# Fewer plain pairs ahead of the seven-product pairs in three SwiGLU layers, and another order of VectorE's list

## The chip, the cores and the metric

The kernel runs on one core of a Trainium2 chip. The metric is the time on the device of one execution, in microseconds (us). Engines are TensorE (PE in the profile), VectorE (DVE), ScalarE (ACT), GpSimd (POOL) and SyncE (SP), which issues the DMAs of the weights.

## What is computed

Two transformer-like blocks over 512 tokens of width 1024, all in float32. Three SwiGLU layers of width 2816 in them take most of the time, and the change touches only those:

```python
def swiglu(x, w_gate, w_up, w_down):
    return (jax.nn.silu(x @ w_gate) * (x @ w_up)) @ w_down

h = h + 0.5 * swiglu(rmsnorm(h, ffn1_norm[l]), ...)   # "g1"
...                                                    # attention branches, gates, projection
h = h + 0.5 * swiglu(rmsnorm(h, ffn2_norm[l]), ...)   # "g2"
...                                                    # convolution and pooling block
h = h + swiglu_2(rmsnorm_2(h, g_ffn[l]), ...)          # "g3"
```

## The kernel before

Each float32 operand is split into a high part (a cast to the rounded type fp32r) and a low part (the value less the high one), and a product is the sum of high x high, low x high and high x low. Weights come in units of 128 x 1024 (one weight chunk for 128 outputs), 512 KB each, through a ring of four slots (`RING`): SyncE loads `raw`, ScalarE casts it to `wh` (`high`, L1204), GpSimd subtracts to `wl` (`low_part`, L487). A slot is loaded again when TensorE has signalled `unit_done` for it.

A layer's gate and up projections have 22 pairs of units (`FC`), one gate and one up unit for each 128 columns. They are done in two ways (`gate_up`):

- The first `PLAINS[name]` pairs are plain: 2 units x 8 chunks x 3 products = 48 matmuls of 512 columns (L620 to L622). VectorE takes the two sums out with `plain_taken` (L1755, L1758), ScalarE does `silu`, VectorE multiplies in `plain_hidden` (L1765).
- The other pairs are mixed: gate and up share seven products instead of eight half-size ones, over combined inputs and combined weights. In `mixed_pair` TensorE does, in order, E, NG, B21, ND, the next pair's B11, B22 and NF, 72 matmuls, 60 of 256 columns and 12 of 512 (L732 to L749). The very first B11 is `first_product`, which stands inside the last plain unit, behind its fifth chunk.

Mixed pairs need combined inputs. For each of four chunks k VectorE makes eight half-width tiles in `mixed_input` (L1773 to L1781), ScalarE casts seven of them (`mixed_input` there, L1329), and VectorE subtracts (`mixed_input_low`, L1786). This is done beside the plain pairs. The combined weights are made pair by pair in VectorE's `frame(p)`: it makes the sums and low parts that pair p+1 needs (L1817, L1819, L1826, L1837, L1844, L1846, L1849, L1858) and puts the products of pair p together (L1823, L1829, L1833, L1840, L1854, L1862). L1840 signals `ff_gate`, without which NF of that pair does not start: its columns of the bank are still being read. `finish` (L1796) makes the hidden chunk. `frame(-1)` stands ahead of the loop and makes the weights of pair 0. ScalarE has a `frame` of its own with the casts and the copies of products (L1334, L1339, L1367); GpSimd does, for each pair, two half-width low parts (`pair_low`, L528, behind L1849) and one quarter (`next_quarter`, L540, behind ScalarE's cast).

Each engine works through its list strictly in the order in which the code writes it; semaphores tie the lists together. There is no planner.

## Time and profile before

| | us |
|---|---|
| median of 3 runs | 1737.55 (1736.27 to 1737.61) |
| profiled execution | 1736.21 |
| its span | 1734.4 |
| mixed part of g1, 16 pairs, first E to the end of the last pair | 77.0 to 235.9 |
| mixed part of g2, 17 pairs | 947.4 to 1116.0 |
| mixed part of g3, 17 pairs | 1431.7 to 1600.5 |

The profiled execution is one run of the program; the profile's times are counted from the start of its span. The granted clock of TensorE was full (0.998 of full speed on the mean). The timeline lists instructions in order of time; a matmul's own duration overlaps the next one's, so the pace of TensorE is read from the distance between starts. The same holds for VectorE to a small extent: instructions of 128 x 512 show 0.68 us and start 0.60 us apart. In brackets stands how long the engine was idle before an instruction and what ended that.

### The profile page before, as it was taken

How to read it: one execution, taken by the hardware profiler on the slowest of the kernel's cores; microseconds unless marked ns; L12 is line 12 of the kernel's file. 1: busy time of each engine (PE TensorE's matmuls, PEld its weight loads, DVE VectorE, ACT ScalarE, POOL GpSimd, SP SyncE). 2: the span in 40 equal slices, each digit the busy share in tenths (PEclk: the TensorE clock that was granted, in tenths of full speed). 3: DMA queues.
4: the chain of work that ended last, by engine and by line, in shares of the span. 5: the costliest groups of instructions: out<-in, count | busy, mean ns of one | idle time of the engine just before them, and what ended most of it. 6: DMA issues, size and time to landing. Idle time of an engine off the chain costs nothing.

```text
span 1734.4 us, 27783 instructions
## 1 busy us (share of the span) xinstructions
PE 1720.8 (99%) x9696; PEld 1454.7 (84%) x9696; DVE 1206.8 (70%) x1809; ACT 876.1 (51%) x1486; POOL 783.0 (45%) x423
## 2 busy tenths in 40 slices
PE   9999999999999999999999999999999999999998
PEld 7899988888888777788888999988866889999887
DVE  6898984278867885236469899843785598998532
ACT  6455552266554477785344555522425445555222
POOL 2344354467565433325453344544533534435443
PEclk9999999999999999999999999999999999999999
DMA  5333333322333221112323333332361323333222
GB/s 178 98 108 102 104 104 96 127 93 88 110 110 113 64 72 50 50 49 86 97 92 95 104 109 104 103 97 97 104 146 61 97 85 107 103 106 109 97 98 73
DMA packets 50518, 168.54 MB, mean 97 GB/s; under 512 B 6264, under 2 KB 7032, under 8 KB 50304
## 3 DMA queue, kind: packets, MB, share of 16 engines
q1 hardware_dynamic: 47088, 161.34, 29.9%
q10 hardware_dynamic: 3344, 6.05, 1.3%
q8 instruction: 55, 0.90, 0.2%
q14 instruction: 31, 0.25, 0.0%
HBM read 161.84 MB, written 2.11 MB: 95 GB/s over the span
## 4 chain that ended last, share of the span: by engine, by line
PE 92%; DVE 4%; issue 2%; ACT 1%; POOL 1%; DMA 0%; POOLq 0%; SPq 0%; ACTq 0%; DVEq 0%
PE bank L620 16%; PE bank L622 16%; PE bank L621 16%; PE bank L746 8%; PE bank L914 7%; PE bank L732 6%; PE bank L734 5%; PE bank L735 5%; PE bank L744 3%; PE bank L959 2%; PE bank L985 2%; PE bank L1087 1%; PE bank L976 1%; PE bank L749 1%; DVE input_low L1691 1%
## 5 line engine op out<-in xcount | busy, mean ns | idle before, releaser
L487 POOL TENSOR_TENSOR weights_low<-raw_weights,weights_high 128x1024 fp32r<-128x1024 f32 x192 | 470.1, 2453 | 558.4 <-ACT weights_high L1204 530.5
L1204 ACT CAST weights_high<-raw_weights 128x1024 fp32r<-128x1024 f32 x244 | 254.1, 1045 | 296.9 <-DMA raw_weights<-weights 278.0
L528 POOL TENSOR_TENSOR weights_low<-raw_weights,weights_high 128x512 fp32r<-128x512 f32 x100 | 149.6, 1518 | 286.4 <-DVE weights_low L1849 286.4
L620 PE MATMUL bank<-input_high,weights_high 128*128 128x512 f32 x624 | 246.2, 395 | 2.4 <-DVE input_low L1691 1.7
L621 PE MATMUL bank<-input_high,weights_low 128*128 128x512 f32 x624 | 243.1, 390 | 0.0
L622 PE MATMUL bank<-input_low,weights_high 128*128 128x512 f32 x624 | 243.1, 390 | 0.0
L732 PE MATMUL bank<-input_mixed,weights_high 128*128 128x256 f32 x600 | 171.9, 287 | 0.0
L735 PE MATMUL bank<-input_mixed,weights_high 128*128 128x256 f32 x600 | 169.2, 282 | 0.0
L746 PE MATMUL bank<-input_mixed,weight_sum_high 128*128 128x512 f32 x400 | 148.9, 395 | 0.0
L620 PEld LDWEIGHTS bank<-input_high,weights_high 128*128 128x128 f32 x624 | 117.2, 188 | 30.7 <-issue 5.0
L622 PEld LDWEIGHTS bank<-input_low,weights_high 128*128 128x128 f32 x624 | 117.1, 188 | 24.8
L621 PEld LDWEIGHTS bank<-input_high,weights_low 128*128 128x128 f32 x624 | 117.2, 188 | 23.2 <-issue 0.2
L1339 ACT CAST weight_sum_high<-weight_sum 128x512 fp32r<-128x512 f32 x150 | 93.3, 622 | 81.7 <-PE bank L746 48.8
L620 PE MATMUL bank<-hidden_high_mid,weights_high 128*128 (+1 forms) x336 | 130.7, 389 | 0.0
L621 PE MATMUL bank<-hidden_high_mid,weights_low 128*128 (+1 forms) x336 | 130.7, 389 | 0.0
L732 PEld LDWEIGHTS bank<-input_mixed,weights_high 128*128 128x128 f32 x600 | 113.8, 190 | 5.0 <-DVE bank L1840 3.1
L735 PEld LDWEIGHTS bank<-input_mixed,weights_high 128*128 128x128 f32 x600 | 114.0, 190 | 0.0
L734 PE MATMUL bank<-input_mixed,weights_low 128*128 128x256 f32 x400 | 113.0, 283 | 0.0
L622 PE MATMUL bank<-hidden_low_first,weights_high 128*128 (+1 forms) x288 | 112.1, 389 | 0.0
L1741 DVE SCALAR_TENSOR_TENSOR residual<-bank,residual 128x512 f32<-128x512 f32 x39 | 26.8, 686 | 108.5 <-PE bank L622 108.4
L1334 ACT COPY product_copies<-bank 128x256 f32<-128x256 f32 x150 | 66.4, 443 | 53.8 <-PE bank L746 47.6
L622 PE MATMUL bank<-hidden_low_rest,weights_high 128*128 128x512 f32 x240 | 93.4, 389 | 0.0
(330 smaller groups left out, 4340.3 us busy)
## 6 DMA issues: line engine op xcount, KB each, us to landing
raw_weights<-weights SPq DMA_DIRECT2D x294, 512.0 KB, 3.6
out_t<-out_t SPq DMA_DIRECT2D x8, 256.0 KB, 2.1
residual<-x_t SPq DMA_DIRECT2D x6, 256.0 KB, 5.9
glu_stacked<-glu_padded ACTq DMA_DIRECT2D x24, 64.0 KB, 4.6
glu_stacked<-glu_padded SPq DMA_DIRECT2D x24, 64.0 KB, 4.7
mem_in<-mem_t ACTq DMA_DIRECT2D x1, 1024.0 KB, 4.9
tile<-forget_sums ACTq DMA_DIRECT2D x4, 256.0 KB, 3.5
raw_weights<-weights SPq DMA_DIRECT2D x3, 256.0 KB, 5.8
```

The lines of the kernel that those rows point to most:

```text
L487: pool.tensor_tensor(wl[:, u % RING, :], raw[:, u % RING, :], wh[:, u % RING, :].bitcast(F32), ALU.subtract).then_inc(low_done, 1)
L528: pool.tensor_tensor(wl[:, u % RING, w], raw[:, u % RING, w], wh[:, u % RING, w].bitcast(F32), ALU.subtract).then_inc(low_done, 1)
L620: pe.matmul(out, wh[:, u % RING, w], rh, start=start, stop=False)
L621: pe.matmul(out, wl[:, u % RING, w], rh, start=False, stop=False)
L622: return pe.matmul(out, wh[:, u % RING, w], rl, start=False, stop=stop)
L732: pe.matmul(out, high[:, w], xmix[k][:, of, 0:HALF], start=first and k == 0, stop=False, skip_group_check=not first)
L734: pe.matmul(out, low[:, w], xmix[k][:, of, 0:HALF], start=False, stop=False, skip_group_check=not first)
L735: mm = pe.matmul(out, high[:, w], xmix[k][:, of, HALF:], start=False, stop=k == 3, skip_group_check=not first)
L746: mm = pe.matmul(out, high[:, w], xmix[k][:, of, :], start=first and k == 0, stop=k == 3, skip_group_check=not first)
L914: mm = pe.matmul(bank[g % 2][:, :], (wl if part == 1 else wh)[:, u % RING, w], (xl if part == 2 else xh)[:, k, :], start=(k == 0 and part ...
L1204: act.copy(wh[:, u % RING, :], raw[:, u % RING, :]).then_inc(high_done, 1)
L1339: act.copy(dst, src).then_inc(sem("sum_high"), 1)
```

## The change

`PLAINS` goes from 6, 5, 5 to 5, 4, 4, so each layer has one plain pair less and one mixed pair more. With four plain pairs `pair_bank` puts the mixed pairs in banks 6/7 and 0/1 in turn (in 0/1 and 2/3 with an odd number, as before), and `first_product` no longer waits for the last `plain_hidden`. The eight tiles of a combined input are put in the order in which TensorE's products use them, and those of chunks 2 and 3 are cast and subtracted in two pieces, `EARLY` (three tiles: B11, E, NG) and `LATE` (four: B21, ND, B22, NF). In g2 and g3 VectorE does the late pieces inside `frame(-1)`, and all of plain pairs 2 and 3 behind it. In the loop the adds that lead to `ff_gate` (L1833, L1829, L1840) move ahead of L1826 and L1837. The diff, cut:

```diff
+PLAINS = {"g1": 5, "g2": 4, "g3": 4}
+EARLY, LATE = slice(0, 3), slice(3, 7)
 HALF = S // 2

-ND_OF, E_OF, NF_OF, NG_OF, B21, B22, B11, B12 = range(8)
+B11, E_OF, NG_OF, B21, ND_OF, B22, NF_OF, B12 = range(8)


 N_GU, N_DN, N_IN, N_BR, N_WO, N_IN2, N_WO2 = 2 * FC, FC, len(IN_STEPS) + GATES, 12, 8, 12, 8
...
+            return 2 * ((n + p) % 2) if n % 2 else 6 * (p % 2 == 0)
+
         def halves_of(tile):
             return tile.rearrange("p (a n) -> p a n", n=HALF)

...
-                pe.wait_ge(sem("xmix_low"), before(name, 4) + 4)
-                pe.wait_ge(sem("ff_hidden"), before(name, FC) + plain - 1)
+                pe.wait_ge(sem("xmix_low"), before(name, 6) + 4)
+                if plain % 2:
+                    pe.wait_ge(sem("ff_hidden"), before(name, FC) + plain - 1)
                 pe.wait_ge(sem("quarter_low"), pairs_before(name, 1) + 1)
-                mixed_product(bank[2 * (plain % 2)][:, 0:HALF], wh[:, up % RING, 0:S], quarter_low, B11).then_inc(sem("products"), 1)
+                mixed_product(bank[pair_bank(name, 0)][:, 0:HALF], wh[:, up % RING, 0:S], quarter_low, B11).then_inc(sem("products"), 1)
...
+                if p == 0:
+                    pe.wait_ge(sem("xmix_low"), before(name, 6) + 6)
                 pe.wait_ge(low_done, at(u + 1, 2))
...
                     high(u, i=i)
+                    if p < 0 and not plain % 2:
+                        mixed_input(3, LATE)
                     if p >= 0:
...
@@ -1387,18 +1399,9 @@
                     mixed_input(1)
                     silu(1)
                     high(u0 + 7)
-                    mixed_input(2)
-                    if plain > 4:
-                        high(u0 + 8)
-                    mixed_input(3)
-                    silu(2)
-                    if plain > 4:
-                        high(u0 + 9)
-                        silu(3)
-                    if plain > 5:
-                        high(u0 + 10)
-                        high(u0 + 11)
-                        silu(4)
+                    mixed_input(2, EARLY)
+                    mixed_input(2, LATE)
+                    mixed_input(3, EARLY)
...
                     high(8)
-                    mixed_input(2)
+                    mixed_input(2, EARLY)
                     high(9)
+                    mixed_input(2, LATE)
+                    mixed_input(3, EARLY)
+                    mixed_input(3, LATE)
                     silu(2)
-                    high(10)
-                    mixed_input(3)
                     silu(3)
-                    high(11)
-                    silu(4)
                 frame(-1)
-                copy_product(copies[:, 0, 0, :], bank[2 * (plain % 2)][:, 0:HALF], 1)
+                copy_product(copies[:, 0, 0, :], bank[pair_bank(name, 0)][:, 0:HALF], 1)
+                if not plain % 2:
+                    silu(plain - 2)
                 silu(plain - 1)
                 looped = mixed // 2 * 2 - 2
...
+                    if p < 0 and not plain % 2:
+                        mixed_input_low(2, 4, LATE)
                     if now:
                         dve.wait_ge(unit_done, at(u0 + 2 * (plain + p) + 1, 2))
                         dve.wait_ge(sem("copied"), at(copied + 3 * p + 1, 3))
                         dve.tensor_tensor(up_out[:, 0:HALF], bank[4][:, 0:HALF], copies[:, c, 0, :], ALU.add
                                           ).then_inc(sem("partial"), 1)
-                    if more:
-                        dve.tensor_tensor(gate[:, 0:S], gate[:, 0:S], up[:, 0:S], ALU.add).then_inc(sem("sums"), 1)
-                    if now:
-                        dve.wait_ge(sem("partial"), at(pairs_before(name, 3) + 3 * p + 1, 3))
-                        dve.tensor_tensor(up_out[:, 0:HALF], bank[4][:, HALF:S], up_out[:, 0:HALF], ALU.add)
-                    if now:
                         dve.wait_ge(sem("products"), at(products + 5 * p + 4, 5))
                         dve.wait_ge(sem("copied"), at(copied + 3 * p + 3, 3))
                         dve.tensor_tensor(bank[b][:, HALF:S], bank[b][:, 0:HALF], copies[:, c, 2, :], ALU.add
                                           ).then_inc(sem("partial"), 1)
+                        dve.wait_ge(sem("partial"), at(pairs_before(name, 3) + 3 * p + 1, 3))
+                        dve.tensor_tensor(up_out[:, 0:HALF], bank[4][:, HALF:S], up_out[:, 0:HALF], ALU.add)
                     if more:
-                        dve.wait_ge(sem("sums"), sum_at(4 * p + 6))
-                        dve.tensor_tensor(s4[:, :], sums[1][:, :], up[:, S:2 * S], ALU.add).then_inc(sem("sums"), 1)
+                        dve.tensor_tensor(gate[:, 0:S], gate[:, 0:S], up[:, 0:S], ALU.add).then_inc(sem("sums"), 1)
                     if now:
                         dve.wait_ge(sem("partial"), at(pairs_before(name, 3) + 3 * p + 2, 3))
                         dve.tensor_tensor(bank[b][:, HALF:S], bank[b][:, HALF:S], copies[:, c, 3, :], ALU.add
                                           ).then_inc(sem("ff_gate"), 1)
                     if more:
+                        dve.wait_ge(sem("sums"), sum_at(4 * p + 6))
+                        dve.tensor_tensor(s4[:, :], sums[1][:, :], up[:, S:2 * S], ALU.add).then_inc(sem("sums"), 1)
                         dve.wait_ge(sem("sum_high"), sum_at(4 * p + 6))
                         dve.tensor_tensor(sum_l[1][:, :], sums[1][:, :], sum_h[1][:, :].bitcast(F32), ALU.subtract
                                           ).then_inc(sem("sum_low"), 1)
                         dve.tensor_tensor(sum_l[0][:, :], sums[0][:, :], sum_h[0][:, :].bitcast(F32), ALU.subtract
                                           ).then_inc(sem("sum_low"), 1)
+                        if p < 0 and not plain % 2:
+                            mixed_input_low(3, 6, LATE)
                         dve.wait_ge(sem("sum_high"), sum_at(4 * p + 7))
                         dve.tensor_tensor(wl[:, (u + 1) % RING, 0:S], gate[:, 0:S], wh[:, (u + 1) % RING, 0:S].bitcast(F32),
                                           ALU.subtract).then_inc(sem("sum_low"), 1)
...
                     plain_taken(1)
                 plain_hidden(1)
                 mixed_input(2)
-                mixed_input_low(1)
+                mixed_input_low(1, 2)
                 if not u0:
                     plain_taken(2)
                 mixed_input(3)
+                mixed_input_low(2, 3, EARLY)
+                mixed_input_low(3, 5, EARLY)
+                if not u0:
+                    mixed_input_low(2, 5, LATE)
+                    mixed_input_low(3, 6, LATE)
+                    plain_hidden(2)
+                    plain_taken(3)
+                    plain_hidden(3)
+                frame(-1)
                 if u0:
                     plain_taken(2)
-                mixed_input_low(2)
-                plain_hidden(2)
-                if not u0:
-                    plain_taken(3)
-                mixed_input_low(3)
-                if not u0:
-                    plain_hidden(3)
-                for c in range(3 if u0 else 4, plain - 1):
-                    plain_taken(c)
-                    plain_hidden(c)
-                frame(-1)
+                    plain_hidden(2)
                 plain_taken(plain - 1)
                 plain_hidden(plain - 1)
                 looped = mixed // 2 * 2 - 2
```

## Rows read from the trace of the kernel before

**Rows 1.** The page, part 1: busy time of each engine, share, instructions.

```profile
PE 1720.8 (99%) x9696; PEld 1454.7 (84%) x9696; DVE 1206.8 (70%) x1809; ACT 876.1 (51%) x1486; POOL 783.0 (45%) x423
```

**Rows 2.** Line L732: what its engine waited for before it: us, times.

```profile
  DVE bank L1840: 3.1, 20
```

**Rows 3.** Timeline, TensorE, first stage: start us, us, engine, line, operation [idle before].

```profile
59.70 0.39 PE L622 MATMUL bank<-input_low,weights_high 128*128 128x512 f32 x1
...
73.30 0.39 PE L622 MATMUL bank<-input_low,weights_high 128*128 128x512 f32 x1
...
73.52 0.28 PE L732 MATMUL bank<-input_mixed,weights_high 128*128 128x256 f32 x1
...
77.01 0.28 PE L732 MATMUL bank<-input_mixed,weight_sum_high 128*128 128x256 f32 x1
```

**Rows 4.** Timeline, TensorE, second stage, columns as in the group above.

```profile
943.88 0.28 PE L732 MATMUL bank<-input_mixed,weights_high 128*128 128x256 f32 x1
...
947.36 0.28 PE L732 MATMUL bank<-input_mixed,weight_sum_high 128*128 128x256 f32 x1
...
955.86 0.28 PE L732 MATMUL bank<-input_mixed,weights_high 128*128 128x256 f32 x1
...
957.29 0.28 PE L732 MATMUL bank<-input_mixed,weight_sum_high 128*128 128x256 f32 x1
...
1105.72 0.30 PE L732 MATMUL bank<-input_mixed,weights_high 128*128 128x256 f32 x1
...
1116.00 0.50 PE L620 MATMUL bank<-hidden_high_first,weights_high 128*128 128x512 f32 x1
```

**Rows 5.** Timeline, VectorE, second stage: last mixed input to the loop.

```profile
926.71 0.74 DVE L1773 SCALAR_TENSOR_TENSOR input_sums<-residual,vectors,bank 128x512 f32<-128x512 f32 x1
...
928.27 2.30 DVE L1777 TENSOR_TENSOR input_sums<-input_sums 128x512 f32<-128x512 f32 x1
...
932.60 2.02 DVE L1786 TENSOR_TENSOR input_mixed<-input_sums,input_mixed 128x1792 fp32r<-128x1792 f32 x1
...
935.13 4.22 DVE L1786 TENSOR_TENSOR input_mixed<-input_sums,input_mixed 128x1792 fp32r<-128x1792 f32 x1
...
947.19 0.68 DVE L1755 TENSOR_TENSOR tile<-bank,token_factor 128x512 f32<-128x512 f32 x1
...
948.57 1.66 DVE L1765 TENSOR_TENSOR hidden_rest<-tile,tile 128x512 f32<-128x512 f32 x1
...
951.31 0.69 DVE L1817 TENSOR_TENSOR weight_sum<-raw_weights 128x512 f32<-128x512 f32 x1 [1.09 <-DMA raw_weights<-weights]
...
954.24 0.68 DVE L1837 TENSOR_TENSOR weight_sum<-weight_sum,raw_weights 128x512 f32<-128x512 f32 x1
...
954.84 0.43 DVE L1840 TENSOR_TENSOR bank<-bank,product_copies 128x256 f32<-128x256 f32 x1
...
1105.09 0.43 DVE L1840 TENSOR_TENSOR bank<-bank,product_copies 128x256 f32<-128x256 f32 x1
```

**Rows 6.** Timeline, GpSimd, the same stretch of the second stage.

```profile
927.62 2.39 POOL L487 TENSOR_TENSOR weights_low<-raw_weights,weights_high 128x1024 fp32r<-128x1024 f32 x1 [4.23 <-ACT weights_high L1204]
...
941.64 1.46 POOL L540 TENSOR_TENSOR quarter_low<-raw_weights,weights_high 128x512 fp32r<-128x512 f32 x1 [4.17 <-ACT weights_high L1204]
...
946.84 2.84 POOL L528 TENSOR_TENSOR weights_low<-raw_weights,weights_high 128x512 fp32r<-128x512 f32 x2 [3.73 <-DVE weights_low L1849]
```

**Rows 7.** Timeline, ScalarE, second stage: one whole cast of a unit.

```profile
940.53 1.03 ACT L1204 CAST weights_high<-raw_weights 128x1024 fp32r<-128x1024 f32 x1
```

**Rows 8.** Timeline, VectorE, first stage, before its first frame.

```profile
50.69 0.74 DVE L1773 SCALAR_TENSOR_TENSOR input_sums<-residual,vectors,bank 128x512 f32<-128x512 f32 x1
...
53.39 2.52 DVE L1779 SCALAR_TENSOR_TENSOR input_sums<-input_sums 128x256 f32<-128x256 f32 x1
...
61.96 2.88 DVE L1765 TENSOR_TENSOR hidden_rest<-tile,tile 128x512 f32<-128x512 f32 x1
...
68.99 0.69 DVE L1817 TENSOR_TENSOR weight_sum<-raw_weights 128x512 f32<-128x512 f32 x1 [2.16 <-DMA raw_weights<-weights]
```

40 lines of the change are left out of this document (21 added, 19 removed).

## The prediction

> **What bounds the kernel now.** I read the busy times first: TensorE 99%, VectorE 70% [rows 1]. The reader is to see that TensorE hardly idles over the whole, so the first question is how many matmuls go. Next I looked at what ended TensorE's idle time at L732, the line that opens NF: VectorE's L1840, 3.1 us in all [rows 2]. Then the timelines of the three places where plain pairs give way to mixed ones. There the share of 70% misleads. In g2 VectorE has no gap from 926.71 until the 1.09 us in front of L1817 at 951.31 [rows 5], while the same stretch of g1 has 2.16 us free in front of its first frame [rows 8]. So each layer's head has two limits, TensorE's matmuls and VectorE's list, and the change moves the first by a whole plain pair.
>
> **Matmul count.** Sixty matmuls of 512 columns start within 73.30 - 59.70 = 13.60 us, 0.2267 each [rows 3]. A plain pair has 48: 10.88 us. A mixed pair takes 957.29 - 947.36 = 9.93 us from E to E where nothing holds it [rows 4]. Each layer swaps one for the other: 0.95 us less, 2.85 us in three layers. Everything ahead of the last plain pair stands as it was, so the first E is wanted 10.88 us earlier.
>
> **The loop.** L1840 falls due once a pair. From its start at 954.84 to 1105.09 are 15 pairs, 10.017 us each [rows 5], against TensorE's 9.93. It is slower from the first pair on, when TensorE doesn't yet wait: L1840(0) ends at 955.27 and NF(0) starts at 955.86 [rows 4, 5]. So VectorE's list has a period of its own, and TensorE runs into it after some six pairs; that gives the 3.1 us. I see what makes it: an instruction of VectorE with two inputs in SBUF doesn't run beside one of GpSimd. L1777, about 0.7 us alone, took 2.30 (to 930.57) while GpSimd's low part ran from 927.62 to 930.01, and L1765 took 1.66, not 0.69, beside `pair_low` [rows 5, 6]. Per pair VectorE gives way to such instructions three times. The new order drops none of these instructions, so I keep 10.017. It does put L1840 ahead of L1837, 0.60 us (954.24 to 954.84) [rows 5]; L1829 and L1833 merely change places with L1826. So `ff_gate` comes 0.60 us sooner once, not in each pair: at most 0.6 per layer. New waits it could bring: L1833 needs ND, which ends 7.1 us after NF starts, about 1 us before VectorE gets there; ScalarE's cast behind L1826 comes 0.66 later, with two more VectorE instructions before its reader L1849. I cost both at nothing in the steady loop, at up to 0.2 us in a layer's first pairs.
>
> **g1.** VectorE between 50.69 and 68.99 [rows 8]: the last mixed input, its low parts, two pairs taken out, one wait. Of these 18.30 us go: 2.16 idle; three instructions of one pair, 1.8 (taken and hidden of pair 4 move behind the frame); 2.1 in L1779 (2.52 against 0.42) and 2.2 in L1765 (2.88 against 0.68), both held by low parts of units 10 and 11, which now are made as quarters and halves; 0.4 in L1777 likewise. Added: two instructions by the splits, 0.14, and a wait of 0.1 for the cast. The frame starts at about 60.5. With one hold of 1.0 by the quarter its fifth instruction ends at about 64.8, before E at 77.01 - 10.88 = 66.13 [rows 3]. The first B11 is due at 73.52 - 10.88 = 62.64, the quarter ends at about 62.45: hidden, with little to spare. So TensorE gains the whole pair: -10.88 + 9.93 - 0.5 (the order: 0.6 less 0.1 for one more pair of the slow period) = **-1.45 us**. If the cover fails by 0.5 us, it is -1.
>
> **g2.** The work is cut in another way here, late pieces in the frame and pairs 2 and 3 behind it, but all of it still lies ahead of `frame(0)`, so the order hardly matters for L1840(0). I sum from 926.71, where nothing has changed, to L1817 of `frame(0)` at 951.31: 24.60 us [rows 5]. Minus 1.8 for one pair taken and hidden (three times 0.60); minus 1.6 in L1777 (2.30 against 0.7) and 2.2 in the second L1786 (4.22 against 2.02), since units 8 and 9 no longer have whole low parts; minus the idle 1.09. Plus 0.14 for two more instructions, 0.1 for a cast, and 1.0 for the next quarter, which now meets VectorE at L1819, as large as the hold of L1765 (1.66 against 0.69) [rows 5]; in the old list it met the idle time. That is 19.15 us: L1817 in effect at 945.86, and L1840 ends 3.53 + 0.43 - 0.60 = 3.36 later, at 949.2. NF(0) is wanted at 955.86 - 10.88 = 944.98 [rows 4]. It is 4.2 us late, and the lateness stays, as VectorE's period is no shorter than TensorE's.
>
> Where TensorE would stand meanwhile: 0.6 at the first B11 (quarter done at 933.6, wanted at 933.0); 0.4 at E (the frame is longer by a late piece, and the copy of B11 waits behind ScalarE's list); 0.8 at B21, which needs GpSimd's half behind L1849, itself behind the second late piece; 3.0 at ND, for a copy that stands in ScalarE's list behind the silu of pair 3 and a cast of 1.03 [rows 7], and that silu waits for VectorE's L1755 at 942.9. The four waits are bounds of the same lateness: together 4.8 us.
>
> End of the layer: before, L1840(15) ends at 1105.52, NF(15) starts 0.20 later, the layer ends 10.28 behind that [rows 4, 5]. Now there are 16 periods behind 949.2: 949.2 + 160.3 = 1109.5, end at 1119.9 against 1116.00: **+4.0 us**. Bounds: if VectorE lost nothing to the quarter and the halves at the start (1.0 each at L1819, at the hidden of pair 2 and at the sum in front), it is 3 less, +1.0; if ScalarE's late copy costs its 4.8 on top of a full loop loss (17 x 0.087 less the 0.5 of slack, 1.0, against 0.9 now), it is 4.8 - 0.95 + 0.1 = +4.0 again; if both chains add a hold of a whole 1.0 and 0.5 more, +5.5. I take +4.0, since each term has a row of the same shape.
>
> The Trainium skill, "SBUF — State Buffer", section "Who interferes with whom", says that VectorE with two SBUF inputs and GpSimd share one pair of ports, and that whoever issues first keeps it for the whole instruction. This trace agrees: L1777 ends 0.56 us after the GpSimd instruction that it waited for [rows 5, 6]. No row shows the other order in the loop, L1817 ahead of the quarter. By the page the quarter would then wait and hold L1819 in its turn, the period would stay at 10.02 and g2 at +4.0; without it g2 could be rival 2's +3.0.
>
> **g3** repeats g2: its last mixed input starts at 1411.03, its L1817 at 1435.72, its first E at 1431.67, distances within 0.1 us of g2's. **+4.0 us** (same bounds).
>
> **Sum.** -1.45 + 4.0 + 4.0 = +6.55 us. Against the profiled execution's 1736.21 (span 1734.4 and 1.8 around it) it gives 1742.8; that execution lies 1.3 below the median, and the median moves to **1744.1 us**, 0.38% slower. A measurement can tell about 0.2% (3.5 us) from no change.
>
> **The rivals.**
> 1. VectorE's head late, as above: 1744.1, within 1741 to 1748. For it: the missing gap in VectorE's timeline. Chance 0.55.
> 2. The same head, but the new order brings the loop's period down to TensorE's 9.93, say because a weight load that lands sooner lets L1817 run before the quarter. Then g2 and g3 end at TensorE's pace behind NF(0) at 949.8: 949.8 + 16 x 9.93 + 10.28 = 1119.0, +3.0 each, and g1 gives -1.95: 1741.6. Against it: the same instructions share the ports whoever goes first. Chance 0.10.
> 3. The holds at the head mostly fall away, because GpSimd's halves and VectorE's instructions pass each other: +1.0 each, 1738.1, no change to be measured. Chance 0.13.
> 4. The other side: VectorE's head isn't what NF(0) waits for. The mechanism would be that the late pieces and the two pairs behind the frame take work out of the path of the first E, and that TensorE's start is all that counts, with `ff_gate` early enough. It decides if L1840(0) ends by 944.98, that is 4.2 us ahead of my sum. Then 2.85 and most of the 3.1 go: 1737.55 - 5.9 = 1731.6, or 1734 with the slow period left. For it: TensorE's first E and B11 are covered nearly in full. Against it: nothing takes VectorE's work away. Chance 0.13.
> 5. Worse: ScalarE's late copy and silus push the loop's first pairs as well, or g1 fails too (its quarter has 0.2 us to spare): +5.5 each and 0 in g1, 1748.5. Chance 0.09.
>
> **How the numbers follow.** Slower by over 0.2%: rivals 1, 2 and 5, less the corner of 1 and 2 near 1741: 0.72. Within 0.2%: rival 3 and that corner: 0.15. Faster: rival 4: 0.13. The range of 8 in 10 goes from rival 3's 1738.0 to 1748.0, near rival 5's; it leaves out rival 4 and part of 5.
>
> **What would show it right or wrong.** Right: in g2 and g3 VectorE without a gap until L1817 of `frame(0)`, and that one starting without a wait for a DMA; L1840(0) near 949 + the 1.45 us that g1 takes off the clock before; TensorE's gaps at ND, B21 and B11 of the first mixed pair, some 4.8 us a layer, with a copy and L1849 as their releasers; L1840 still 10.02 apart; g1 with no gap at its first B11 and E, its mixed part at 168 to 169 us. Wrong: a gap on VectorE in front of `frame(0)`, or L1840 less than 9.95 apart, or first mixed pairs of 9.93 us in g2. My sum would fail first if a hold by GpSimd falls elsewhere than I put it, since these are 1 us apiece and six of them stand in it.

## The result and the profile after

The changed kernel takes 1744.13 us (median of 5 runs, 1743.52 to 1746.64), the kernel before beside it 1737.28 (5 runs, 1735.66 to 1737.61). The ratio is 1.0045 [1.0034, 1.0057], so it is 6.85 us slower; the forecast was 1744.1, in a range of 1738.0 to 1748.0. The profiled execution took 1743.5 (span 1741.6), TensorE's clock 0.998 of full on the mean.

The page, part 1, of the kernel after (answers to [rows 1]):

```profile
PE 1719.7 (99%) x9768; PEld 1455.8 (84%) x9768; DVE 1242.1 (71%) x1851; ACT 884.6 (51%) x1513; POOL 782.5 (45%) x426
```

TensorE is busy 1.1 us less in a span that is 7.2 us longer. What L738 (L732 before) waited for, us and times, answers to [rows 2]; this list counts a matmul and its weight load both:

```profile
  ACT product_copies L1344: 11.9, 6
...
  DVE bank L1842: 1.6, 10
  POOL quarter_low L546: 1.3, 4
```

VectorE's L1842 (L1840 before), which led the list with 3.1, has sunk to 1.6; in front stands a copy of ScalarE that wasn't there at all. Timeline of TensorE, second stage (answers to [rows 4]): first B11, E, B21, ND, NF, the second pair's E, the end of the layer.

```profile
932.62 0.36 PE L738 MATMUL bank<-input_mixed,weights_high 128*128 128x256 f32 x1 [0.49 <-POOL quarter_low L546]
...
936.35 0.39 PE L738 MATMUL bank<-input_mixed,weight_sum_high 128*128 128x256 f32 x1
...
940.11 0.50 PE L752 MATMUL bank<-input_mixed,weights_high 128*128 128x512 f32 x1 [0.67 <-POOL weights_low L534]
...
944.38 0.39 PE L738 MATMUL bank<-input_mixed,weights_high 128*128 128x256 f32 x1 [2.61 <-ACT product_copies L1344]
...
948.73 0.28 PE L738 MATMUL bank<-input_mixed,weights_high 128*128 128x256 f32 x1
...
950.17 0.28 PE L738 MATMUL bank<-input_mixed,weight_sum_high 128*128 128x256 f32 x1
...
1119.21 0.50 PE L626 MATMUL bank<-hidden_high_first,weights_high 128*128 128x512 f32 x1 [0.37 <-DVE hidden_low_first L1917]
```

From E to E the first pair takes 950.17 - 936.35 = 13.82 us, where [rows 4] has 9.93. The same in the first stage (answers to [rows 3]), where nothing waits:

```profile
63.12 0.28 PE L738 MATMUL bank<-input_mixed,weights_high 128*128 128x256 f32 x1
...
66.61 0.28 PE L738 MATMUL bank<-input_mixed,weight_sum_high 128*128 128x256 f32 x1
```

VectorE, second stage (answers to [rows 5]). From 925.69 to L1822 (L1817 before) of `frame(0)` no instruction waits for anything:

```profile
925.69 0.74 DVE L1777 SCALAR_TENSOR_TENSOR input_sums<-residual,vectors,bank 128x512 f32<-128x512 f32 x1
...
927.25 0.69 DVE L1781 TENSOR_TENSOR input_sums<-input_sums 128x512 f32<-128x512 f32 x1
...
931.36 1.67 DVE L1824 TENSOR_TENSOR weight_sum<-weight_sum,raw_weights 128x512 f32<-128x512 f32 x1
...
940.21 1.65 DVE L1769 TENSOR_TENSOR hidden_rest<-tile,tile 128x512 f32<-128x512 f32 x1
941.78 0.68 DVE L1759 TENSOR_TENSOR tile<-bank,token_factor 128x512 f32<-128x512 f32 x1
...
943.77 0.68 DVE L1822 TENSOR_TENSOR weight_sum<-raw_weights 128x512 f32<-128x512 f32 x1
944.49 1.66 DVE L1824 TENSOR_TENSOR weight_sum<-weight_sum,raw_weights 128x512 f32<-128x512 f32 x1
...
947.67 0.42 DVE L1842 TENSOR_TENSOR bank<-bank,product_copies 128x256 f32<-128x256 f32 x1
...
1098.04 0.42 DVE L1842 TENSOR_TENSOR bank<-bank,product_copies 128x256 f32<-128x256 f32 x1
```

The three of 1.65 to 1.67 us, otherwise 0.69, meet a GpSimd instruction and wait for it, which is called a hold below: a quarter, `pair_low` and a quarter. The last two lines are 15 periods of 10.025 us. ScalarE at the same place: the silu of pair 3, which waits for VectorE's L1759, then a whole cast and the two copies that ND waits for.

```profile
942.49 0.63 ACT L1335 ACTIVATE tile<-tile 128x512 f32<-128x512 f32 x1 [2.32 <-DVE tile L1759]
943.03 1.03 ACT L1214 CAST weights_high<-raw_weights 128x1024 fp32r<-128x1024 f32 x1
943.96 0.85 ACT L1344 COPY product_copies<-bank 128x256 f32<-128x256 f32 x2
```

Where the time went, by the distance between the ends of the layers' mixed parts:

| stretch | before | after | difference | forecast |
|---|---|---|---|---|
| first plain unit of g1 to its end | 207.35 | 206.17 | -1.18 | -1.45 |
| end of g1 to end of g2 | 880.13 | 884.04 | +3.91 | +4.0 |
| end of g2 to end of g3 | 484.51 | 488.36 | +3.85 | +4.0 |

The first plain unit itself started 0.48 later in this execution (29.00 against 28.52), ahead of all that was changed. The three rows sum to +6.58. The row of g2 holds 0.32 us that were gained between the layers, where nothing was changed: g1 ended 0.70 earlier than before, g2's last mixed input (L1777 at 925.69, L1773 at 926.71) came 1.02 earlier. Counted from that instruction, g2 costs 4.23 us; g3, in the same way, 3.89.

### The profile page after: what moved, and what is told of

It reads as the page before. It is cut to its first block, busy times and chain, and to the rows that moved or that the text cites. A ratio compares the mean times of both kernels' runs of the same rounds, so it can differ in the third digit from the quotient of the medians.

```text
span 1741.6 us, 28200 instructions
## 1 busy us (share of the span) xinstructions
PE 1719.7 (99%) x9768; PEld 1455.8 (84%) x9768; DVE 1242.1 (71%) x1851; ACT 884.6 (51%) x1513; POOL 782.5 (45%) x426
## 4 chain that ended last, share of the span: by engine, by line
PE 88%; DVE 7%; issue 2%; ACT 1%; POOL 1%; DMA 0%; POOLq 0%; SPq 0%; ACTq 0%
PE bank L626 14%; PE bank L627 14%; PE bank L628 14%; PE bank L752 8%; PE bank L924 8%; PE bank L738 6%; PE bank L740 6%; PE bank L741 6%; PE bank L750 3%; PE bank L969 2%; PE bank L995 2%; PE bank L1097 1%; PE bank L986 1%; PE bank L755 1%; DVE input_low L1695 1%
## 5 line engine op out<-in xcount | busy, mean ns | idle before, releaser
L493 POOL TENSOR_TENSOR weights_low<-raw_weights,weights_high 128x1024 fp32r<-128x1024 f32 x186 | 455.5, 2453 | 532.0 <-ACT weights_high L1214 503.3
L534 POOL TENSOR_TENSOR weights_low<-raw_weights,weights_high 128x512 fp32r<-128x512 f32 x106 | 158.6, 1517 | 300.9 <-DVE weights_low L1855 300.9
L626 PE MATMUL bank<-input_high,weights_high 128*128 128x512 f32 x576 | 227.5, 395 | 2.8 <-DVE input_low L1695 2.2
L627 PE MATMUL bank<-input_high,weights_low 128*128 128x512 f32 x576 | 224.5, 390 | 0.0
L628 PE MATMUL bank<-input_low,weights_high 128*128 128x512 f32 x576 | 224.4, 390 | 0.0
L738 PE MATMUL bank<-input_mixed,weights_high 128*128 128x256 f32 x636 | 181.9, 286 | 6.2 <-ACT product_copies L1344 5.2
L741 PE MATMUL bank<-input_mixed,weights_high 128*128 128x256 f32 x636 | 179.4, 282 | 0.0
L752 PE MATMUL bank<-input_mixed,weight_sum_high 128*128 128x512 f32 x424 | 157.9, 395 | 0.0
L626 PEld LDWEIGHTS bank<-input_high,weights_high 128*128 128x128 f32 x576 | 108.2, 188 | 29.0 <-issue 5.5
L738 PEld LDWEIGHTS bank<-input_mixed,weights_high 128*128 128x128 f32 x636 | 120.6, 190 | 11.8 <-ACT product_copies L1344 5.9
L628 PEld LDWEIGHTS bank<-input_low,weights_high 128*128 128x128 f32 x576 | 108.1, 188 | 23.0
L741 PEld LDWEIGHTS bank<-input_mixed,weights_high 128*128 128x128 f32 x636 | 120.7, 190 | 0.0
```

Source lines behind the costliest of these rows:

```text
L493: pool.tensor_tensor(wl[:, u % RING, :], raw[:, u % RING, :], wh[:, u % RING, :].bitcast(F32), ALU.subtract).then_inc(low_done, 1)
L534: pool.tensor_tensor(wl[:, u % RING, w], raw[:, u % RING, w], wh[:, u % RING, w].bitcast(F32), ALU.subtract).then_inc(low_done, 1)
L626: pe.matmul(out, wh[:, u % RING, w], rh, start=start, stop=False)
L627: pe.matmul(out, wl[:, u % RING, w], rh, start=False, stop=False)
L628: return pe.matmul(out, wh[:, u % RING, w], rl, start=False, stop=stop)
L738: pe.matmul(out, high[:, w], xmix[k][:, of, 0:HALF], start=first and k == 0, stop=False, skip_group_check=not first)
```

## The experiments

The kernel before, run beside them, had a median of 1736.81 (beside order_only, old_order, five and five_quarter), 1737.3 (beside after_quarter, thin_quarter, more_vector and head_before_frame) and 1736.98 (beside the other four). Where a stage is named, the numbers are distances as in the table above.

**order_only** is the kernel before with the new list in the loop alone: the adds that lead to `ff_gate` ahead of L1826 and L1837.

```diff
                     if more:
-                        dve.wait_ge(sem("sums"), sum_at(4 * p + 6))
-                        dve.tensor_tensor(s4[:, :], sums[1][:, :], up[:, S:2 * S], ALU.add).then_inc(sem("sums"), 1)
+                        dve.tensor_tensor(gate[:, 0:S], gate[:, 0:S], up[:, 0:S], ALU.add).then_inc(sem("sums"), 1)
                     if now:
                         ...
                                           ).then_inc(sem("ff_gate"), 1)
                     if more:
+                        dve.wait_ge(sem("sums"), sum_at(4 * p + 6))
+                        dve.tensor_tensor(s4[:, :], sums[1][:, :], up[:, S:2 * S], ALU.add).then_inc(sem("sums"), 1)
```

> The kernel before with the new order of VectorE's list in the loop alone (plain pairs 6, 5, 5). My theory: the order gives 0.6 us once per layer and leaves L1840's period at 10.02 us, so TensorE's waits at L732 fall from 3.1 to about 1.3 us and the time by 1.8 us, to 1735.5. Rival: the order brings the period to TensorE's 9.93, all waits go, minus 3.1 us. Second rival: a new wait at L1833 eats the gain, no change.

Measured: 1736.13 us (11 runs), ratio 0.9996 [0.9987, 1.0005]. End of g1 to end of g2: 0.32 shorter, g2 to g3: equal. The period of `ff_gate` stays at 10.01 to 10.05 but for single pairs. NF of g2 begins to wait at about the ninth pair, not the sixth, so the list does give the slack of 0.6, but 0.3 of it is lost again at a B11 for which the quarter came late, in a pair where the weight sum went ahead of it. In g1 the weights for the second frame landed 1.4 later, VectorE was late from there, and the stretch from the first E to the end of the layer is 1.03 longer than before; why the weights landed later isn't shown. VectorE's timeline, order_only:

```profile
82.45 0.69 DVE L1817 TENSOR_TENSOR weight_sum<-raw_weights 128x512 f32<-128x512 f32 x1 [3.38 <-DMA raw_weights<-weights]
```

From the first E to the layer's end g2 is 0.16 shorter and g3 equal. Up to the last E they gain 0.25 and 0.33; from there to the end they lose 0.09 and 0.33, for a reason shown below with the forecast's term for the list. So the list is worth 0 to 0.2 a layer here, less than the forecast's 0.6.

**old_order** is the other half: the kernel after with the old list, so the edit above the other way round.

> The changed kernel with the old order in the loop. My theory: g2 and g3 each end 0.6 us later and g1 0.5, since VectorE's list bounds them, so plus 1.7 us on the changed kernel, 1745.8. Rival (order pays nothing where the head is late): 1744.1. Second rival (order changes the period): plus 3 or more.

Measured: 1746.14 us (5 runs), ratio 1.0053 [1.004, 1.0067], 2.0 above the kernel after. g1 ends 0.28 later and g2 to g3 is 0.54 longer, at full clock: that is the list's share (0.45 in either from the first E to the end). g1 to g2 is 1.5 longer, and there TensorE's clock fell. Windows from ND of the first mixed pair to the second E, in g2 and in g3: length, busy time of PE, PEld, DVE, ACT and POOL, then the granted clock:

```profile
944.77:952.07 7.30, 7.30 (x44) 7.13 (x45) 6.96 (x13) 3.70 (x7) 2.25 (x2) 0.77 0.06 25
1434.77:1440.67 5.90, 5.90 (x44) 5.60 (x45) 5.87 (x11) 3.60 (x7) 1.23 (x1) 1.00 0.10 37
```

The same 44 matmuls take 7.30 at 0.77 and 5.90 at 1.00, 0.12 of which is a wait for VectorE.

**five** leaves five plain pairs in g2 and g3 too, with the split inputs and the new list; pairs 2 to 4 and the late pieces stand as in g1, ahead of the frame for pairs 2 and 3 (VectorE's list is changed in the same way as ScalarE's, shown here).

```diff
-PLAINS = {"g1": 5, "g2": 4, "g3": 4}
+PLAINS = {"g1": 5, "g2": 5, "g3": 5}
...
+                    high(u0 + 8)
                     mixed_input(3, EARLY)
+                    mixed_input(3, LATE)
+                    silu(2)
+                    high(u0 + 9)
+                    silu(3)
```

> The changed kernel with five plain pairs in all three layers: g2 and g3 go back to five, with the split inputs and the new order, g1 stays at five. My theory: the loss of the change is all in going to four pairs in g2 and g3; here g1 keeps its 0.7 us and g2 and g3 gain 0.6 each by the order: 1735.4, that is 8.7 below the changed kernel. Rival: the split of the casts costs by itself in g2 and g3: 1737 or more.

Measured: 1734.58 us (11 runs), ratio 0.9987 [0.9978, 0.9996], g1 to g2 0.24 and g2 to g3 0.26 shorter than before. All of the loss is in going to four plain pairs; with five, g1 keeps its gain and VectorE waits 1.13 (g2) and 0.91 (g3) for a DMA ahead of `frame(0)` again. From the first E to the end g2 and g3 are 0.11 longer and 0.20 shorter than before, so the split inputs and the new list together change little there.

**five_quarter** adds to five one wait on GpSimd: the quarter goes behind VectorE's weight sum instead of ahead of it.

```diff
+                        pool.wait_ge(sem("sums"), pairs_before(name, 4) + at(4 * q + 1, 8))
                         pool.tensor_tensor(quarter_low[:, :], ...
```

> As the run with five pairs in all layers, and GpSimd's quarter waits for L1822 of the same frame, so that VectorE's first sum always takes the ports ahead of it. In the changed kernel's trace that happened twice by chance, and the period of L1842 was 9.82 there, not 10.02. My theory: period below 9.93 in every pair, TensorE's waits at NF go, minus 1.2 more: 1734.2. Rival: B11 then waits for the quarter in every pair, some 0.3 us each, plus 10 us or more. Second rival: the two short periods were chance, no change against 1735.4.

Measured: 1787.69 us, ratio 1.0296 [1.0282, 1.031]. The theory fell. The waits close a ring through four lists: NF frees a weight slot, the DMA fills it, the sum waits for the DMA, the quarter for the sum, B11 for the quarter, NF stands behind B11. Timelines of VectorE, GpSimd and TensorE, five_quarter:

```profile
181.32 0.69 DVE L1828 TENSOR_TENSOR weight_sum<-raw_weights 128x512 f32<-128x512 f32 x1 [2.11 <-DMA raw_weights<-weights]
182.09 1.77 POOL L547 TENSOR_TENSOR quarter_low<-raw_weights,weights_high 128x512 fp32r<-128x512 f32 x1 [2.90 <-DVE weight_sum L1828]
184.00 0.38 PE L739 MATMUL bank<-input_mixed,weights_high 128*128 128x256 f32 x1 [1.14 <-POOL quarter_low L547]
```

A pair then takes 10.9 to 11.4 us, 11.1 on the mean. **after_quarter** puts the same wait into the kernel after; it was meant to tell whether the quarter ahead of the sum costs VectorE its hold:

> The changed kernel with GpSimd's quarter behind L1822 of its frame. My theory: the head stays late by 4 us in g2 and g3, but the loop no longer loses to VectorE's period: minus 0.9 in g2 and g3 each, minus 0.5 in g1: 1741.8. Rival: B11 waits for the quarter, slower than 1744.1; in the head the quarter is late already, so it could cost up to 0.6 once in each layer.

Measured: 1796.86 us (4 runs), ratio 1.0342 [1.0324, 1.0359], the same ring: 10.7 to 11.3 us a pair, 11.0 to 11.1 on the mean of a layer. Neither run says what a hold costs.

**thin_quarter** does say it: all quarters but the first of each layer are cut to 8 columns, so most of that low part is left out of the output.

```diff
-                    pool.tensor_tensor(quarter_low[:, :], raw[:, u % RING, 0:S], ...
+                    n = 8 if q else S
+                    pool.tensor_tensor(quarter_low[:, 0:n], raw[:, u % RING, 0:n], ...
```

> The changed kernel, but every quarter except a layer's first is made over 8 columns instead of 512, so its low part is left out of the output. It takes one of GpSimd's three holds out of each pair. My theory (VectorE gives way to GpSimd's whole instruction): L1824 of frame(0) in g2 takes 0.69, not 1.66, L1842 is no longer the slower one and comes at TensorE's 9.93, and the time falls by some 2.3 us to 1741.8 (0.9 in g2 and g3, 0.5 in g1), no further, because ND of the first mixed pair still waits for ScalarE's copy. Rival (the period has another cause, say the weights' DMA): period 10.02 and 1744.1.

Measured: 1743.04 us (6 runs), ratio 1.0031 [1.0018, 1.0043]. The loop's period drops to 9.94 and g1 ends at 234.07, 1.1 earlier than after. In g2 and g3 the first L1825 after the head takes 0.69, not 1.66, yet the layers are no shorter than after's (884.21 and 488.72 against 884.04 and 488.36). In g2, from E to ND it is the same 8.02 as after's 8.03, since ND's copy waits for silu(3); from ND to the second E it is 1.50 more, at a fallen clock; from there to the end 1.29 less (167.75 against 169.04), of which 0.95 goes at NF in the loop and 0.34 behind the last E. Timeline, TensorE, and the two windows from ND to the second E, thin_quarter:

```profile
943.24 0.39 PE L739 MATMUL bank<-input_mixed,weights_high 128*128 128x256 f32 x1 [2.59 <-ACT product_copies L1345]
```

```profile
943.24:950.53 7.29, 7.29 (x44) 7.12 (x45) 6.02 (x13) 3.60 (x7) 0.89 (x2) 0.77 0.05 16
1431.95:1439.25 7.30, 7.30 (x44) 7.12 (x45) 5.64 (x13) 3.51 (x7) 0.43 (x2) 0.77 0.08 30
```

So two limits must be told apart, VectorE's list (V) and ScalarE's copy for ND (S). In the kernel after L1842(0) ends at 948.09 and NF starts at 948.73: `ff_gate` was ready 0.64 before NF, where an NF that waits for it starts 0.05 to 0.08 behind it. So this NF came late by TensorE's chain through ND; waiting for VectorE alone, it could have started some 0.6 sooner.

**more_vector** puts more of VectorE's instruction L1762 of `plain_taken` into the list: three in g2's third plain pair, one in g3's fourth and one in g1's fifth.

```diff
+                    for _ in range({("g1", 4): 1, ("g2", 2): 3, ("g3", 3): 1}.get((name, c), 0)):
+                        own(dve.tensor_tensor(tiles[2 + p][:, :], bank[2 * p + 1][:, :], rstd[:, :], ALU.mult))
```

> The changed kernel with VectorE instructions added that write nothing new (a copy of L1762 with a wait, about 0.72 us each, none with two SBUF inputs): three in g2 at the third plain pair, one in g3 at the fourth, one in g1 at the fifth. My theory (VectorE's list ahead of frame(0) sets the end of g2 and g3, and g1 has 0.87 us to spare): g2 plus 2.2, g3 plus 0.7, g1 nothing: 1747.0. Rival (TensorE's or ScalarE's waits at the head set it): less than half of that.

Measured: 1748.66 us (4 runs), ratio 1.006 [1.0043, 1.0077]. g1 is the same to 0.02, so VectorE has room there. g1 to g2 grew by 3.6, g2 to g3 by 1.23. The three took 2.13 us, but `plain_hidden(2)` came out of step with GpSimd and lost its hold of 1.0, so silu(3) and ND came only 1.22 later after E; another 2.37 went between ND and the second E, at a clock of 0.67. In g3 ND came no later after E (8.03), and between ND and the second E went 1.30, at a clock of 0.80. So the 2.2 and 0.7 that were expected of VectorE's list aren't seen: at equal clock it is 1.2 and nothing, and the run doesn't tell V from S. Timelines, VectorE and TensorE, and the window from ND to the second E, more_vector:

```profile
939.70 2.13 DVE L1763 TENSOR_TENSOR tile<-bank,token_factor 128x512 f32<-128x512 f32 x3
...
942.66 0.69 DVE L1771 TENSOR_TENSOR hidden_rest<-tile,tile 128x512 f32<-128x512 f32 x1
```

```profile
945.87 0.58 PE L738 MATMUL bank<-input_mixed,weights_high 128*128 128x256 f32 x1 [3.83 <-ACT product_copies L1344]
```

```profile
945.87:954.03 8.16, 8.16 (x44) 7.98 (x45) 6.98 (x13) 3.71 (x7) 2.06 (x2) 0.67 0.01 2
```

**head_before_frame** tests the forecast's sentence that the order of the head hardly matters: in g2 and g3 late pieces and pairs 2 and 3 go ahead of `frame(-1)`, on VectorE and on ScalarE.

```diff
-                frame(-1)
                 if u0:
                     plain_taken(2)
-                    plain_hidden(2)
-                plain_taken(plain - 1)
-                plain_hidden(plain - 1)
+                plain_hidden(2)
+                plain_taken(3)
+                plain_hidden(3)
+                frame(-1)
```

> The changed kernel with g2's and g3's heads in g1's arrangement: late pieces and plain pairs 2 and 3 ahead of frame(-1), nothing in or behind it; counts unchanged. My theory (the order of the head hardly matters for L1842 of frame(0), only its sum does): the first E is late by 5 us instead of none, ND no longer is, L1842 of frame(0) lies within 1 us of its place, and the time within 1.5 us of 1744.1. Rival (the late pieces and the pairs behind the frame are what keeps the loss small): plus 3 us or more for each of the two layers, 1750.

Measured: 1764.69 us (4 runs), ratio 1.0156 [1.0139, 1.0173]: 10.5 us a layer, and the sentence fell for the pairs. Not all of it is waiting: behind the waits of 6.53 and 5.03 the granted clock was 0.61 to 0.65 and then, in the first mixed pair, 0.83 to 0.85, and the matmuls took 4.2 us longer in g2 and 3.6 in g3 than the same ones before. ScalarE's cast for the quarter now stands behind silu(3), the quarter comes late, B11 stands in TensorE's list inside the last plain unit, and VectorE waits for that unit's bank before it makes the frame. Timelines of GpSimd, TensorE, VectorE and TensorE again, head_before_frame:

```profile
937.07 1.26 POOL L546 TENSOR_TENSOR quarter_low<-raw_weights,weights_high 128x512 fp32r<-128x512 f32 x1 [14.89 <-ACT weights_high L1214]
```

```profile
938.48 0.55 PE L738 MATMUL bank<-input_mixed,weights_high 128*128 128x256 f32 x1 [6.53 <-POOL quarter_low L546]
...
949.33 0.58 PE L738 MATMUL bank<-input_mixed,weight_sum_high 128*128 128x256 f32 x1 [5.03 <-ACT product_copies L1344]
```

```profile
944.34 0.69 DVE L1762 TENSOR_TENSOR tile<-bank,token_factor 128x512 f32<-128x512 f32 x1 [8.94 <-PE bank L628]
```

**late_ahead** moves the late pieces alone ahead of `frame(-1)`.

```diff
+                mixed_input_low(2, 5, LATE)
+                mixed_input_low(3, 6, LATE)
                 if not u0:
-                    mixed_input_low(2, 5, LATE)
-                    mixed_input_low(3, 6, LATE)
```

> The changed kernel, in g2 and g3 with the late pieces ahead of the first frame and only the plain pairs 2 and 3 behind it. A smaller test of the claim that the order of the head does not matter, after the arrangement with everything ahead of the frame cost 10 us a layer through a ring: pair 3 was awaited by the frame, and its last unit held the product that waited for the frame's cast. Here no ring: the first B11 starts 1 us later, E 1 us later, B21 as before, L1842 of frame(0) at its place within 0.3 us, and the time is the same, 1744. Rival: the late pieces inside the frame save what they shift, plus 1 us a layer.

Measured: 1744.29 us (4 runs), ratio 1.0039 [1.0023, 1.0054], as the kernel after. g2 to g3 is 0.33 longer at full clock; g1 to g2 is 1.46 longer, with a granted clock of 0.77 from ND to the second E. B11 and E come 0.5 and 1.2 later, the wait at ND is 0.2 shorter: the time is moved within the head. The 1 us a layer of the rival isn't there.

**taken_first** takes pair 3 out of its banks before `plain_hidden(2)`, so that silu(3) and the copy behind it come sooner, with the same number of instructions.

```diff
                     plain_taken(2)
-                    plain_hidden(2)
                 plain_taken(plain - 1)
+                if u0:
+                    plain_hidden(2)
                 plain_hidden(plain - 1)
```

> The changed kernel, in g2 and g3 with plain pair 3 taken out (L1759, L1762) ahead of the hidden of pair 2, so that ScalarE's silu of pair 3, its next cast and its copy come some 1.5 us sooner. VectorE's list keeps its sum. Theory V (VectorE's list sets the end of the layer): ND of the first mixed pair starts 1.5 us sooner, but L1842 of frame(0) stays at its place, 0.6 us ahead of NF before, and the layers end within 0.3 us of where they did: 1744. Rival S (ScalarE's late copy sets it): each of the two layers ends 1.5 us sooner, 1741.

Measured: 1740.11 us (11 runs), ratio 1.0016 [1.0007, 1.0025]; g1 to g2 1.43 and g2 to g3 1.16 shorter than after. The wait at ND goes from 2.61 to 0.86, but VectorE's end moved as well. Timelines of VectorE and of TensorE, taken_first:

```profile
940.96 1.27 DVE L1769 TENSOR_TENSOR hidden_rest<-tile,tile 128x512 f32<-128x512 f32 x2
...
946.07 0.42 DVE L1842 TENSOR_TENSOR bank<-bank,product_copies 128x256 f32<-128x256 f32 x1
```

```profile
942.36 0.38 PE L738 MATMUL bank<-input_mixed,weights_high 128*128 128x256 f32 x1 [0.86 <-ACT product_copies L1344]
```

Two of `plain_hidden` in 1.27 us, where one alone took 1.65: the hold by `pair_low` is gone, and L1842(0) comes 1.3 sooner against E. The run lands nearer S's 1741 than V's 1744, but both limits moved, so the total doesn't tell them apart. The stretches say more: from the first E to the end g2 is 1.45 and g3 1.22 shorter than after, near VectorE's 1.3 and not the copy's 1.75; NF(0) now starts 0.3 later against ND, and from the sixth pair on g2's TensorE waits for L1842.

**thin_taken** does both, thin quarters and pair 3 taken first.

> The thin quarters (8 columns behind a layer's first, so a low part is left out of the output) together with pair 3 taken out first. In the run with thin quarters alone TensorE's granted clock was 0.77 in the first mixed pair of g2 and g3, behind its wait at ND, and that hid what the quarters give. With the wait 1.5 us shorter I expect a clock of 1.00 there, L1843's period at TensorE's 9.93, and now the 1.3 us a layer of VectorE's period as well as the shorter head: g2 and g3 2 us each sooner than in the changed kernel, 1739.5. Rival: the clock falls here too, 1742.

Measured: 1736.43 us (10 runs), ratio 0.9996 [0.9987, 1.0005], better than the 1739.5 expected; g1 to g2 and g2 to g3 are 3.0 and 2.83 shorter than after, the period is 9.93 to 9.94, and the clock doesn't fall. Against taken_first that is 1.6 a layer in g2, 0.3 of it ahead of the second E and 1.29 behind it. So in the square of four (1744.1 after; 1743.0 thin; 1740.1 taken; 1736.4 both) thin quarters give 1.29 behind the second E with and without the swap, and the head nothing by themselves but 0.3 with the swap; the swap gives the head 1.75 up to ND in either case; and thin alone loses 1.5 again by the clock.

**five_gate_first** is five with L1842's add moved one place further ahead, before the add of the gate weights.

```diff
                                           ).then_inc(sem("ff_gate"), 1)
                     if more:
+                        dve.tensor_tensor(gate[:, 0:S], gate[:, 0:S], up[:, 0:S], ALU.add).then_inc(sem("sums"), 1)
+                    if more:
```

> The run with five plain pairs in all layers, and in the loop the add that signals ff_gate also ahead of the sum of the raw weights (L1845 behind L1848). My theory: ff_gate comes 0.6 us sooner once per layer, TensorE's remaining 0.8 us of waits at NF goes: 1733.9 against 1734.6. Rival: ScalarE's cast and copies behind that sum come 0.6 later and hold E of the next pair: no gain or slower.

Measured: 1734.13 us (11 runs), ratio 0.9982 [0.9973, 0.9991], the fastest of all and 10.0 below the kernel after. What L738 waited for, us and times:

```profile
...
  POOL quarter_low L546: 0.8, 3
```

VectorE is no longer in it, though its period is still 10.03: `ff_gate` of g2's first pair is ready at 953.39 for NF at 954.83, and each pair eats 0.1 of these 1.44 us. They don't run out (0.47 is the least in any layer), also because one pair in each layer is shorter by 0.2 on VectorE; but its B11 waits for the quarter there, and those pairs take TensorE 10.27 to 10.46 instead of 9.93. Against five the medians differ by 0.45, less than the intervals tell.

## Why the prediction was right, and where its steps were off

The mechanism was right: one plain pair less makes VectorE's list late at the head of g2 and g3, TensorE stands there for 4.8 us a layer, and g1 has room. That the total agrees so closely is luck: the three stretches were off by +0.27, -0.09 and -0.15 us, g2's row holds 0.32 that g2 didn't gain, the medians moved by 6.85 and five executions of the kernel lie 3.1 apart.

**Matmul count.** Right. In g1 the E of the first mixed pair comes 77.01 - 66.61 = 10.40 earlier, and 10.88 from the first plain unit's start, as summed.

**g1.** -1.18 against -1.45. B11 came at 62.64 by the clock of before (63.12 less the late start of 0.48), the forecast to the hundredth. The frame with its one hold is there too. VectorE, first stage (answers to [rows 8]):

```profile
60.92 0.68 DVE L1822 TENSOR_TENSOR weight_sum<-raw_weights 128x512 f32<-128x512 f32 x1
61.64 1.67 DVE L1824 TENSOR_TENSOR weight_sum<-weight_sum,raw_weights 128x512 f32<-128x512 f32 x1
...
70.76 0.83 DVE L1822 TENSOR_TENSOR weight_sum<-raw_weights 128x512 f32<-128x512 f32 x1 [0.87 <-DMA raw_weights<-weights]
```

VectorE waits 0.87 ahead of `frame(0)`: g1 still has room, g2 none. The term that was off is the new list's, -0.5: it is -0.36 up to the last E, where 0.2 went at one B11 (202.02, its quarter late), and +0.12 behind it.

**The new list's price, left out of the forecast.** The forecast took the layer's end as it was, 10.28 us behind the last NF. From the last E to the end of the layer it was 8.81 to 8.83; it is 8.93, 9.15 and 9.16 in g1, g2 and g3. In the new list VectorE's L1855, for which `pair_low` waits, starts 2.14 behind L1842, where L1849 started 1.54 behind L1840. GpSimd's work behind it comes later, its whole low part runs until 1118.60, and the first split of the hidden activations starts at 1118.14 and is held; the first matmul behind the layer waits 0.37 for it. Timelines of GpSimd and VectorE of the kernel after, and of VectorE before:

```profile
1116.20 2.40 POOL L493 TENSOR_TENSOR weights_low<-raw_weights,weights_high 128x1024 fp32r<-128x1024 f32 x1
1118.14 1.02 DVE L1917 TENSOR_TENSOR hidden_low_first<-hidden_first,hidden_high_first 128x512 fp32r<-128x512 f32 x1
```

```profile
1115.26 0.68 DVE L1912 TENSOR_TENSOR hidden_low_first<-hidden_first,hidden_high_first 128x512 fp32r<-128x512 f32 x1
```

Before, the same low part ended at 1115.14, just ahead. old_order, with the list of before, has 8.82 to 8.83 again, and so has thin_quarter (8.81), where VectorE isn't late.

**g2 and g3, VectorE's sum.** Right in size. By the clock of before (L1773 at 926.71, now 925.69, so 1.02 on top) L1842(0) ends at 949.11; the forecast was 949.2. Its parts are all there: L1781 at 0.69 without its hold, the low parts' holds gone, no wait for the DMA, one more hold at L1824. The Trainium skill, "SBUF — State Buffer", section "Who interferes with whom", says that whichever of the two issues first keeps the ports for its whole instruction. The trace agrees, also in the order for which the forecast had no row: in g1 of the kernel after L1822 ran at 200.12 ahead of the quarter (200.15, 1.81 where it takes 1.28 to 1.31 in most pairs), and the quarter held L1824 in its turn, for 1.66. But the period didn't stay at 10.02, as the forecast worked out for this order: it is 9.81 in that pair, and 9.83 and 9.84 in the other three such pairs of this kernel and order_only. So rival 2's mechanism is worth 0.2 where it occurs. It occurs up to three times in a run, and B11 then comes late for its quarter, by 0.2 in this kernel.

**TensorE's waits.** Forecast 0.6 at B11, 0.4 at E, 0.8 at B21, 3.0 at ND, 4.8 together. Measured 0.64, 0.25, 0.83 and 2.87, with 0.2 in first matmuls: NF(0) starts at 949.75 by the clock of before, 4.77 later than 944.98. The releasers are those named: quarter, `pair_low` behind L1855, ScalarE's copy.

**Which of the two bounds.** The forecast put VectorE first (NF 4.2 late) and called the four waits bounds of the same lateness. At NF(0) ScalarE's copy for ND came last, by 0.6: without the hold at L1824 the head was no shorter (thin_quarter, E to ND). That copy in turn stands behind the silu of pair 3, which waited 2.32 for VectorE's L1759, so both limits come from the one late list. The end of the layer is VectorE's, as forecast: by the clock of before L1842(0) comes 6.16 before L1840(0) did (949.11 against 955.27), one period more makes it 3.86 late, and from the eighth pair on g2's NF starts 0.05 to 0.08 behind `ff_gate` until the sixteenth. No run made the copy alone sooner, so what that would give isn't shown. Both sums agree: 4.78 of waits - 0.95 + 0.08 in the loop + 0.32 at the layer's end is g2's 4.23; in g3 it is 4.77 - 0.95 - 0.26 + 0.33 = 3.89, with one of the shorter pairs.

**The loop.** The period of 10.017 is 10.025. The slack of 0.64 at its start is eaten in seven pairs; the forecast's loss was 0.9 to 1.0 a layer, and g2's NF waits come to 0.96. Two of the forecast's readings need a correction. VectorE gives way twice in a pair, not three times: at L1864 (1.75) and at L1822; of the two halves of `pair_low` the second takes 1.75 instead of 1.30 itself. And its list isn't full: before, it idled 0.4 to 1.1 us in each pair of g2 in front of L1817, waiting for a DMA, at the same period. What repeats is a ring of VectorE and GpSimd. Timelines of both, second stage of the kernel after:

```profile
999.93 0.68 DVE L1855 TENSOR_TENSOR weights_low<-raw_weights,weights_high 128x512 fp32r<-128x512 f32 x1
1000.78 3.00 POOL L534 TENSOR_TENSOR weights_low<-raw_weights,weights_high 128x512 fp32r<-128x512 f32 x2 [5.77 <-DVE weights_low L1855]
1003.74 1.29 POOL L546 TENSOR_TENSOR quarter_low<-raw_weights,weights_high 128x512 fp32r<-128x512 f32 x1
1003.92 1.66 DVE L1822 TENSOR_TENSOR weight_sum<-raw_weights 128x512 f32<-128x512 f32 x1
...
1009.96 0.68 DVE L1855 TENSOR_TENSOR weights_low<-raw_weights,weights_high 128x512 fp32r<-128x512 f32 x1
```

L1855 takes 0.68, the quarter starts 3.12 behind its end, behind `pair_low` in GpSimd's list, and takes 1.29; L1822, wherever it starts, ends 0.55 behind the quarter; 4.38 later the next L1855 starts. That is 10.02 us, and these five numbers are the same to 0.02 in most pairs of before, order_only, old_order and five, while L1822 takes from 0.69 to 1.85. The three orders of the list that were tried keep the same instructions between L1822 and L1855, and so keep the period; a quarter of 8 columns (thin_quarter) or a sum that goes ahead of its quarter opens the ring. Whether an add moved behind L1855 would shorten it wasn't tried.

**The head's order.** The step that failed, without weight in the sum. It holds for the late pieces (0.3 a layer at equal clock). It doesn't for the plain pairs: 10.5 a layer in a ring (some 4 of them at a fallen clock), and 1.2 to 1.4 to gain by a swap of two steps.

**The rivals.** Rival 4 fell: nothing takes VectorE's or ScalarE's work away at the head. Rival 3 fell as well, since a hold of 1.0 was there at each of the three places. Rival 5's place was right, ScalarE's late copy, and its +5.5 is what g2 shows where the clock falls too (old_order: 3.91 + 1.5).

## What to carry to other kernels

Where one kind of work gives way to another, write down for each engine when its last instruction ends and when its reader wants it, and shorten the first kind only as far as the latest of them allows: here five plain pairs covered the work of VectorE and ScalarE, and four did not: 4.8 us of waits a layer for 0.95 saved. When a loop is slower than its busiest engine, look for a ring of two engines that hold and await each other before you reorder one list. When two limits lie within a microsecond, relieve each alone and both together, and read the stretches, not the total: a clock that falls behind a wait can hide the gain. Before an instruction is put behind another in a list, or a wait between two, follow the waits round: if they come back to the same list through a freed buffer and its DMA, the loop runs at the ring's pace (11.1 us instead of 10.02).

## What the runs showed of the hardware that was not expected

TensorE's clock. Behind the wait at ND, of 2.4 to 2.6 us, the granted clock of the next 44 matmuls (45 in late_ahead and after_quarter) was 0.77 of full (the mean over both of its levels, 1.2 and 2.4 GHz) in thin_quarter (both layers) and in g2 of old_order, late_ahead and after_quarter, 0.80 in more_vector's g3 and 0.67 in its g2, there behind 3.83. It was 1.00 in the kernel after in both layers, behind the same 2.61, and in g3 of old_order, late_ahead and after_quarter. It costs 1.5 us at 0.77 and 2.4 at 0.67. Windows from ND to the second E of the kernel after, g2 and g3, columns as above:

```profile
944.38:950.17 5.79, 5.79 (x44) 5.61 (x45) 5.76 (x11) 3.61 (x7) 1.22 (x1) 1.00 0.08 30
1432.88:1438.66 5.78, 5.78 (x44) 5.61 (x45) 5.75 (x11) 3.61 (x7) 1.23 (x1) 1.00 0.07 28
```

Behind a wait of 0.86 (taken_first, thin_taken) it stayed full. What decides between fall and none behind equal waits stays open. And a hold isn't a fixed price of an instruction: three more instructions in front of `plain_hidden(2)`, or a swap, took its hold of 1.0 away, so 2.13 us of work added on VectorE delayed ND by 1.22.
